# GpSimd issues the loads of the first three sample states ahead of its subtractions for the input projection

## The chip, the cores and the metric

The kernel runs on one core of a Trainium2 chip. The metric is the device time of one execution in microseconds; the time of a kernel is the median of its runs. The engines of the core are TensorE (PE; its weight loads are PEld), VectorE (DVE), ScalarE (ACT), GpSimd (POOL) and SyncE (SP). SP and GpSimd issue the transfers: SP's go through the DMA queue q1, GpSimd's through q0, and both queues are served by the same 16 DMA engines.

## What is computed

One inference step of a two-layer decoder for a prompt of 256 tokens and 8 sample tokens, 264 tokens in all, in float32. The part that matters here is the first layer's mLSTM mixer:

```python
proj = x @ w_in + b_in
x_m, o_pre, i_pre, f_pre = jnp.split(proj, [A_INNER, 2 * A_INNER, 2 * A_INNER + A_HEADS], axis=-1)
x_c = silu(causal_conv(x_m))                      # 4 taps along the tokens
q, k = x_c @ w_q[h], x_c @ w_k[h] * A_HEAD_DIM ** -0.5
v = x_m @ w_v[h]
log_i, log_f = i_pre, log_sigmoid(f_pre)
h, C, n, m = mlstm_chunkwise(q, k, v, log_i, log_f, C0, n0, m0)   # C <- decay * C + (ws * k)^T v
h = sigmoid(o_pre) * h
return h @ w_out, new_conv, C, n, m
```

A_INNER is 2048, there are 4 heads of 512. Each of the 8 sample tokens brings its own matrix memory C0 for each head: 32 states of 512x512 float32, 1 MB each, which are read, decayed, updated and written back. The second layer is sliding-window attention, and both layers end in a large mixture of experts (PEER), which takes most of the span.

## The kernel before

All weights that are streamed lie in HBM as units of 128 x 1024 float32 (512 KB). SP loads them in order into a ring of four buffers (`raw`): the first four at once, each further one when the unit four places earlier has been used (L380). Between the first four and the loop, SP issues x (after the first unit), then the inputs of the gate products (w_gate, b_gate, m_in, sel4, sel8: L362, five transfers on one semaphore, gate_in), then const, cols, cols_a, conv_in and some small ones.

Units 0 to 31 are the input projection. For each of them ScalarE rounds the weights to a high part (L862), GpSimd subtracts to get the low part (the function `lows`, L1608; two subtractions of 128x512 a unit), and TensorE does three products a chunk (high by high, high by low, low by high). After units 0 and 1 TensorE does the 32 products for the gates (L558), which wait for gate_in. ScalarE then computes the gate values (L996 to L1001), VectorE scans them (from L1388), and then does the convolution over the x_m channels (L1411, L1413), chunk by chunk as the projection delivers them.

Units 32 to 37 belong to head 0 and are used as plain float32 by TensorE: 32 to 35 hold W_q and W_k, 36 and 37 the two halves of W_v (`project_v`). Unit 36 is issued by SP when unit 32 has been used, 37 when 33 has, and so on. After them TensorE goes on with the prompt's scores and the steps over the sample states (`sample_step`), which ScalarE decays first (L1064).

GpSimd's program is one sequence. Before the change: the 64 subtractions of `lows(U_IN, U_QKV)`, the loads of states 0 to 2 (L1613) into the buffer `cs` (part of `big`), the store of the new m (L1615), the store of the convolution's tail (L1617), the store of the rows of the attention's relative bias to HBM, each row repeated 128 times (`bias_rows`, L1620, 3 MB), which waits until VectorE has written them (bias_rows_kept, L1423), the loads of states 3 and 4 into `halves` (L1624), which wait for the last use of the split weights, and then the loop over the 32 states (L1629, L1638). Nothing else uses `cs` before the loads.

Of the kernel before, what the change touches and what calls it, by code (L numbers as in the profile page):

```python
# [59 lines left out]
U_IN = 0  # L60
U_QKV = U_IN + 2 * IC
# [26 lines left out]
def n_split(n):  # L88
    return _before(n, "pool", "dve")
# [41 lines left out]
def _build(nc, io, ctx):  # L131
# [5 lines left out]
    def sem(name):  # L137
        if name not in sems:
            sems[name] = ctx.enter_context(nc.semaphore(name))
        return sems[name]  # L140
# [5 lines left out]
    sizes = [("big", n_big), ("raw", RING * 1024), ("halves", 4096), ("xh", n_x), ("xl", n_x), ("scb", 4096),  # L146
             ("top", 528 + 2 * 256 + 2 * 128 + 384 + 768), ("const", NCONST), ("cols", NCOLS)]
    total = sum(n for _, n in sizes)
    sb("arena", [P, total])
    base = nc.sbuf_base - 4 * total  # L150
# [1448 lines left out]
    def _(pool):  # L1599
        def lows(a, b):  # L1600

            n0 = n_split(a)
            with pool.Fori(0, (b - a) // RING) as it:
                for k in range(RING):
                    for half in range(2):
                        v, o = 2 * ((n0 + k) % 2) + half, slice(half * 512, (half + 1) * 512)
                        pool.wait_ge(high_done, it * (2 * RING) + (2 * (n0 + k) + half + 1))
                        nc.gpsimd.tensor_tensor(split[:, v, 1, :], ring[:, (a + k) % RING, o], split_f[:, v, 0, :],  # L1608
                                                ALU.subtract).then_inc(low_done["pool"], 1)

        lows(U_IN, U_QKV)
        for n in range(3):
            pool.dma_start(cs[:, n], io["state_in"][n]).then_inc(sem(f"state_in_{n}"), 16)  # L1613
        pool.wait_ge(sem("m_kept"), 1)
        pool.dma_start(io["m_out"], m_out[0:HA, :]).then_inc(sem("small_out"), 16)  # L1615
        pool.wait_ge(sem("conv_kept"), 1)
# [216 lines left out]
```

## Time and profile before

| | us |
|---|---|
| median of 3 runs | 2440.13 |
| lowest run | 2440.05 |
| the profiled execution, its own time | 2439.59 |
| its span, from the first to the last instruction | 2437.8 |
| TensorE busy | 2311.4 (95%) |
| VectorE busy | 1576.5 (65%) |
| ScalarE busy | 1136.2 (47%) |
| GpSimd busy | 918.6 (38%) |

In the profile, times are microseconds from the start of the span, those of single instructions ns where marked. The granted clock of TensorE is given as a share of full speed: 1.00 is 2.4 GHz and 0.50 is 1.2 GHz. Engine names with a q (SPq, POOLq) are an engine's queue of instructions, where DMA issues are counted.

### The profile page before, as it was taken

The page shows a single profiled execution, that of the slowest core. Times are in us where ns is not written, and L with a number is a line of the kernel's source. Part 1 is how long each engine was busy: PE and PEld are TensorE (multiplying, and loading weights), DVE is VectorE, ACT ScalarE, POOL GpSimd, SP SyncE. Part 2 cuts the span into 40 slices and gives each one's busy share as a digit, 9 for nine tenths or more (in the row PEclk, how much of TensorE's full clock was granted, in tenths as well). Part 3 has the DMA queues.
Part 4 walks back from the last instruction along what each step waited for, and adds up shares of the span by engine and source line. Part 5 has one row for each costly group of instructions (what it writes and reads, how often), then busy time and mean ns, then how long its engine had stood idle before and what let it go on. Part 6 is the DMA issues. An engine that isn't in the chain of part 4 may idle for free.

```text
span 2437.8 us, 51606 instructions
## 1 busy us (share of the span) xinstructions
PE 2311.4 (95%) x17330; PEld 2141.1 (88%) x17330; DVE 1576.5 (65%) x3494; ACT 1136.2 (47%) x2231; POOL 918.6 (38%) x754
## 2 busy tenths in 40 slices
PE   7889999989999999999999888899989999999997
PEld 6854555789999999999999877899989999999997
DVE  6404544319996999755555644189969997555555
ACT  5523333156654444455555542556544444555554
POOL 5621111077976666200000150779866662000000
PEclk9999999999999999999999988999989999999999
DMA  4487777544544444455555631545434444555552
GB/s 159 138 235 306 296 296 293 194 161 147 181 164 138 138 138 138 143 180 179 179 180 181 198 126 66 164 147 182 167 130 138 138 138 143 180 179 180 180 180 103
DMA packets 105491, 420.81 MB, mean 173 GB/s; under 512 B 12101, under 2 KB 12701, under 8 KB 95945
## 3 DMA queue, kind: packets, MB, share of 16 engines
q1 hardware_dynamic: 92728, 335.28, 40.9%
q0 software_dynamic: 12400, 83.47, 9.8%
q8 instruction: 45, 0.74, 0.1%
q10 hardware_dynamic: 288, 1.08, 0.1%
q14 instruction: 30, 0.25, 0.0%
HBM read 375.14 MB, written 44.63 MB: 172 GB/s over the span
## 4 chain that ended last, share of the span: by engine, by line
PE 76%; DVE 17%; issue 3%; POOL 2%; ACT 1%; DMA 1%; POOLq 0%; ACTq 0%; DVEq 0%; SPq 0%
PE pa L390 48%; PE pb L390 27%; DVE top L1220 4%; DVE top L1217 3%; POOL split L1608 2%; DVE pa L1260 1%; DVE pa L1259 1%; DVE top L1262 1%; DVE scb L1223 1%; DMA raw<-in_units 1%; DVE pb L1223 1%; DVE scb L1237 0%; DVE big L1437 0%; DVE top L1239 0%; DVE top L1256 0%
## 5 line engine op out<-in xcount | busy, mean ns | idle before, releaser
L862 ACT CAST split<-raw 128x512 fp32r<-128x512 f32 x1176 | 721.0, 619 | 928.0 <-PE pa L390 650.0
L390 PE MATMUL pa<-xh,split 128*128 128x264 f32 x5280 | 997.4, 288 | 64.1 <-DVE xl L1202 23.9
L1608 POOL TENSOR_TENSOR split<-raw,split 128x512 fp32r<-128x512 f32 x664 | 869.8, 1320 | 328.6 <-ACT split L862 306.8
L390 PEld LDWEIGHTS pa<-xh,split 128*128 128x128 f32 x5280 | 836.1, 191 | 69.6 <-POOL split L1608 30.1
L390 PE MATMUL pa<-xl,split 128*128 128x264 f32 x2640 | 755.5, 286 | 0.0
L1209 DVE TENSOR_TENSOR split<-raw,split 128x512 fp32r<-128x512 f32 x512 | 354.3, 693 | 302.3 <-ACT split L862 302.3
L390 PEld LDWEIGHTS pa<-xl,split 128*128 128x128 f32 x2640 | 506.0, 192 | 0.0
L390 PE MATMUL pa<-wsplit,split 128*128 128x264 f32 x3072 | 416.6, 285 | 6.6 <-DVE wsplit L1355 6.6
L390 PE MATMUL pb<-wsplit,split 128*128 128x264 f32 x3072 | 415.0, 284 | 0.0
L390 PEld LDWEIGHTS pa<-wsplit,split 128*128 128x128 f32 x3072 | 391.9, 189 | 6.9 <-issue 6.9
L390 PEld LDWEIGHTS pb<-wsplit,split 128*128 128x128 f32 x3072 | 390.9, 188 | 0.0
L1303 DVE TENSOR_SCALAR scb<-pa,top 128x128 f32<-128x128 f32 x528 | 173.6, 397 | 0.0
L1318 DVE TENSOR_TENSOR big<-big,top 128x264 f32 (+1 forms) x128 | 144.0, 1125 | 39.7 <-ACT top L921 26.1
L390 PE MATMUL pa<-big,raw 128*128 128x264 f32 x640 | 150.4, 390 | 2.5 <-ACT big L1048 1.7
L390 PEld LDWEIGHTS pa<-big,raw 128*128 128x128 f32 x640 | 119.6, 190 | 37.0 <-issue 16.6
L1657 POOL DMA_DIRECT2D big<-in_kw_in x1 | 1.2, 1195 | 388.3 <-DVE big L1182 388.3
L390 PE MATMUL pb<-scb 128*128 128x128 f32 (+2 forms) x1080 | 133.9, 276 | 0.0
L390 PEld LDWEIGHTS pb<-scb 128*128 128x128 f32 (+1 forms) x1080 | 127.2, 191 | 1.2 <-issue 0.9
L1355 DVE TENSOR_TENSOR wsplit<-big,wsplit 128x264 fp32r<-128x264 f32 x256 | 109.3, 427 | 1.1 <-ACT wsplit L970 1.1
L970 ACT CAST wsplit<-big 128x264 fp32r (+1 forms) x256 | 104.6, 409 | 6.0 <-DVE big L1311 6.0
L390 PE MATMUL pb<-big 128*128 128x128 f32 (+6 forms) x514 | 101.3, 369 | 3.8 <-ACT big L911 3.2
L390 PEld LDWEIGHTS pb<-big 128*128 128x128 f32 (+3 forms) x514 | 67.1, 181 | 39.8 <-issue 31.4
(238 smaller groups left out, 1655.9 us busy)
## 6 DMA issues: line engine op xcount, KB each, us to landing
raw<-in_units SPq DMA_DIRECT2D x636, 512.0 KB, 3.3
big<-in_state_in POOLq DMA_DIRECT2D x20, 1024.0 KB, 8.1
out_state_out<-big POOLq DMA_DIRECT2D x20, 1024.0 KB, 5.3
halves<-in_state_in POOLq DMA_DIRECT2D x12, 1024.0 KB, 9.0
out_state_out<-halves POOLq DMA_DIRECT2D x12, 1024.0 KB, 5.2
out_c_prompt<-big POOLq DMA_DIRECT2D x4, 1024.0 KB, 5.1
bias_rows<-scb POOLq DMA_DIRECT2D x1, 3072.0 KB, 39.3
big<-in_skeys POOLq DMA_DIRECT2D x2, 1024.0 KB, 6.8
```

The source lines that it names most:

```text
L390: return pe.matmul(out, lhs, rhs, start=start, stop=stop)
L862: nc.scalar.copy(split[:, 2 * (n % 2) + half, 0, :], ring[:, slot, half * 512:(half + 1) * 512]).then_inc(high_done, 1)
L970: nc.scalar.copy(wsplit[:, i % 4, 0, :], big[:, bass.ds(it * (4 * T) + i * T, T)] if it is not None else w3[:, i, :]).then_inc(sem("w_high ...
L1209: V.tensor_tensor(split[:, 2 * (n % 2) + half, 1, :], ring[:, slot, o], split_f[:, 2 * (n % 2) + half, 0, :], ALU.subtract).then_inc(low_d ...
L1217: last = V.max(s[:, o], v)
L1220: last = V.max_index(i[:, o], s[:, o], v)
L1223: last = V.match_replace(v, s[:, o], v, LOWEST)
L1259: link(V.tensor_tensor(eq, rank.to_broadcast([n, nk, TOPK]), i16, ALU.is_equal))
L1303: last = V.tensor_scalar(hot[:, s % 2, 0, t, :], iota_p, i_col, g_col, ALU.is_equal, ALU.mult)
L1318: V.tensor_tensor(w, w, gelu[:, i % RING, :], ALU.mult).then_inc(sem("row_gated"), 1)
L1355: V.tensor_tensor(wsplit[:, i % 4, 1, :], big[:, bass.ds(it * (4 * T) + i * T, T)], wsplit_f[:, i % 4, 0, :], ALU.subtract).then_inc(sem(" ...
L1608: nc.gpsimd.tensor_tensor(split[:, v, 1, :], ring[:, (a + k) % RING, o], split_f[:, v, 0, :], ALU.subtract).then_inc(low_done["pool"], 1)
```

## The change

The loop that issues the loads of states 0 to 2 moves from behind the 64 subtractions to the head of GpSimd's program. Its three DMAs, their targets and their semaphores stay the same, and no wait is added or taken away.

```diff
-        lows(U_IN, U_QKV)
         for n in range(3):
             pool.dma_start(cs[:, n], io["state_in"][n]).then_inc(sem(f"state_in_{n}"), 16)
+        lows(U_IN, U_QKV)
         pool.wait_ge(sem("m_kept"), 1)
         pool.dma_start(io["m_out"], m_out[0:HA, :]).then_inc(sem("small_out"), 16)
```

On GpSimd, at the head of its program (the memsets of constants at L1801 come first, the branch and the ISA instruction at L1603 open the loop of `lows`):

```order
 L1801 MEMSET const-uint8-127 128x1
 L1598 UNCONDITIONAL_BRANCH
+L1612 DMA big<-in_state_in 128x2048 x3
 L1603 UNCONDITIONAL_BRANCH
 L1603 ISA
```

The three loads stand ahead of the loop with the subtractions, right behind the constants. At the other end of that loop, where the input projection hands over to the heads:

```order
 L1603 REGISTER_ALU
 L1603 COMPARE_AND_BRANCH
-L1613 DMA big<-in_state_in 128x2048 x3
 L1615 DMA out_m_out<-big 4x9
 L1617 DMA out_conv_out<-big 128x432
```

The stores of m and of the convolution's tail, and after them that of the bias rows, now follow the last subtraction directly. The order on the other four engines is the same.

## Rows read from the trace of the kernel before

**Rows 1.** The page, busy time of each engine (share of the span) and instructions.
```profile
PE 2311.4 (95%) x17330; PEld 2141.1 (88%) x17330; DVE 1576.5 (65%) x3494; ACT 1136.2 (47%) x2231; POOL 918.6 (38%) x754
```

**Rows 2.** The chain of work that ended last, 130 to 520 us: start, length, what.
```profile
145.79 21.04 DMA raw<-in_units
```

**Rows 3.** Timeline of PE, 154 to 178: start, length, instruction, [idle before <-releaser].
```profile
154.20 5.72 PE L390 MATMUL pb<-raw,big 128*128 128x512 f32 x12
166.88 8.55 PE L390 MATMUL pb<-raw,big 128*128 128x512 f32 x12 [6.96 <-DMA raw<-in_units]
```

**Rows 4.** Busy time by stretch; the last columns are granted clock, DMA share, GB/s.
```profile
165.00:170.00 5.00, 3.12 (x4) 1.18 (x4) 0.00 (x0) 0.00 (x0) 0.00 (x0) 0.50 0.99 171
```

**Rows 5.** Timeline of GpSimd, 130 to 140.
```profile
133.28 1.75 POOL L1613 DMA_DIRECT2D big<-in_state_in  x3
135.02 0.52 POOL L1615 DMA_DIRECT2D out_m_out<-big  x1
...
136.79 1.05 POOL L1620 DMA_DIRECT2D bias_rows<-scb  x1 [0.70 <-DVE scb L1423]
137.83 1.06 POOL L1624 DMA_DIRECT2D halves<-in_state_in  x2
```

**Rows 6.** Issues of L1613 with times to landing; DMA issues, 133 to 152, bias_rows (landing last).
```profile
L1613 POOL DMA_DIRECT2D big<-in_state_in x3: 527/546/699, 133.3 to 134.5; - x3
...
DMA to landing us min/median/max: 6.3/8.1/10.7
...
bias_rows<-scb POOLq DMA_DIRECT2D x1, 3072.0 KB, 39.3
```

**Rows 7.** DMA issues at 141.4, 145.8 and 150.2 (units 36, 37, 38): us to landing last.
```profile
raw<-in_units SPq DMA_DIRECT2D x1, 512.0 KB, 10.5
...
raw<-in_units SPq DMA_DIRECT2D x1, 512.0 KB, 21.0
...
raw<-in_units SPq DMA_DIRECT2D x1, 512.0 KB, 23.8
```

**Rows 8.** DMA queues, 152 to 158, then 158 to 166: packets, MB, share of engines.
```profile
q0 software_dynamic: 130, 0.60, 96.4%
q1 hardware_dynamic: 4, 0.02, 0.7%
...
q0 software_dynamic: 164, 0.76, 80.2%
q1 hardware_dynamic: 157, 0.58, 17.8%
```

**Rows 9.** Busy time by stretch, columns as in rows 4 (GB/s last).
```profile
2.00:12.00 10.00, 4.15 (x19) 4.18 (x20) 4.37 (x12) 4.83 (x13) 4.54 (x4) 1.00 1.01 378
136.00:145.00 9.00, 8.43 (x45) 7.00 (x44) 0.65 (x4) 1.06 (x3) 2.20 (x4) 1.00 1.00 385
```

**Rows 10.** SP's issues of const and cols_a at the start, and their times to landing.
```profile
5.15 0.36 SPq L363 DMA_DIRECT2D const<-in_const  x1
...
const<-in_const SPq DMA_DIRECT2D x1, 192.0 KB, 6.9
...
6.04 0.45 SPq L365 DMA_DIRECT2D big<-in_cols_a  x1
...
big<-in_cols_a SPq DMA_DIRECT2D x1, 124.0 KB, 6.4
```

**Rows 11.** Timeline of all engines, 0 to 30.
```profile
4.64 2.48 POOL L1608 TENSOR_TENSOR split<-raw,split 128x512 fp32r<-128x512 f32 x2 [4.18 <-ACT split L862]
...
6.75 2.60 ACT L903 CAST xh<-big 128x264 fp32r<-128x264 f32 x8 [1.67 <-DMA big<-in_x]
...
14.07 0.46 ACT L1022 ACTIVATE big<-pa,big 128x256 f32<-128x256 f32 x1
...
15.78 7.28 PE L390 MATMUL pb<-big 128*4 128x264 f32 x32
```

**Rows 12.** Timeline of VectorE, 26 to 35.
```profile
26.75 0.42 DVE L1388 SCALAR_TENSOR_TENSOR scb<-scb 4x264 f32<-4x264 f32 x1 [13.36 <-ACT scb L1001]
```

**Rows 13.** Busy time in the convolution's stretch: PE, PEld, DVE, ACT, POOL.
```profile
34.60:91.50 56.90, 39.90 (x292) 38.60 (x290) 53.47 (x68) 34.13 (x87) 33.39 (x24) 0.93 0.36 120
```

**Rows 14.** Timeline of ScalarE, 118 to 200: the first decay of a state.
```profile
154.96 2.00 ACT L1064 ACTIVATE big<-big 128x2048 f32<-128x2048 f32 x1
```

## The prediction

> **What bounds the kernel now.** I read the page first: TensorE is busy 95% of the span, so microseconds are lost only where it stands still or runs at its half clock [rows 1]. The change touches two stretches, the first 25 us and the hand-over from the input projection to the heads of the mLSTM (133 to 182 us), so I read these from the chain of waits, the timelines and the packets of the two DMA queues.
>
> In the second stretch the chain holds one wait for a transfer: a weight unit issued at 145.79 that lands 21.04 us later [rows 2]. Units 0 to 31 are the input projection, 32 to 35 hold W_q and W_k of head 0, 36 and 37 its W_v. TensorE runs unit 36 from 154.20 in 5.72 us, stands still for 6.96 us for unit 37, and then needs 8.55 us for the same twelve instructions [rows 3], because the granted clock is at its lower level, 0.50 (1.2 GHz), after the stand [rows 4]. The place costs 6.96 + (8.55 - 5.72) = 9.8 us. That is the most that any edit here can win.
>
> Why unit 37 is late: GpSimd issues 3 state loads from 133.28, the broadcast of bias rows at 136.79, and two more state loads [rows 5]. The three states take until 134.5 + 10.7 = 145.2, and bias_rows until 136.8 + 39.3 = 176.1, so it has the engines for 30.9 us behind the states [rows 6]. Unit 36, issued at 141.4, lands after 10.5 us; unit 37 after 21.0; unit 38, issued at 150.2, after 23.8, which is 7.2 us behind unit 37 [rows 7]. From 152 to 158 the queue of the units (q1) moves 4 packets and GpSimd's (q0) 130, though unit 37 had been issued at 145.8; from 158 to 166 they move 157 and 164 [rows 8]. So a unit issued into a backlog of bias_rows waits some 12 us for its first packet and then shares the engines packet by packet.
>
> **The change, part by part.**
>
> *The loads at the start.* Three DMAs of 1024 KB are 3.15 MB. The engines are full from 2 to 12 us at 378 GB/s, and the same loads ran at 385 GB/s at 136 to 145 [rows 9]; both show 16 engines at their limit, so all that stands behind the loads in a queue is put off by 3.15 MB / 0.385 MB per us = 8.2 us. If part of the SP queue gets past, it is less; I take 7.9 and keep 7.5 to 8.3. Who is hit? The inputs of the gate products stand in the SP queue just ahead of const, which is issued at 5.15 and lands after 6.9, so at 12.05 at the latest [rows 10]. TensorE starts the 32 gate products at 15.78 and needs 7.28 us [rows 11]: 3.7 us are spare. 12.05 + 7.9 = 19.95, so the gate products begin 4.2 us later (3.8 to 4.6).
>
> What else is late lies under that wait. x lands near 6.7, when ScalarE starts on it [rows 11]; if it shares its last half with a state, it comes some 2 us later, and units 0 and 1 end at 15.8 + 2 = 18, still ahead of 19.95. cols_a, issued at 6.04 with 6.4 us to landing, goes from 12.4 to 20.3 [rows 10]; ScalarE's first evacuation at 14.07 [rows 11] then comes at 20.3, and what it has left ahead of the gates is two pairs of casts and evacuations, a few us, done before the gate products end at 27.2. GpSimd's issue work, 133.28 to 135.02 for three, 1.75 us [rows 5], falls into the 4.18 us for which it waits before its first subtraction at 4.64 [rows 11].
>
> Is the 4.2 us given back later? VectorE waits 13.36 us for the gate values and only then goes on to the scans and the convolution [rows 12]; from 34.6 to 91.5 it is busy 53.47 of 56.9 us while TensorE is busy 39.9 [rows 13]. The stage is VectorE's, it starts from the gates, and it has no slack. The cost is carried in full. Whether TensorE loses its clock over 1.7 to 4 us of standing there, no row settles; nothing is the lower bound and 2.83 us (the price in rows 3) the upper one, and I take nothing.
>
> *The place the loads leave.* GpSimd gets to its stores 1.75 us sooner, but bias_rows waits for VectorE (0.70 us before it in rows 5) and is still issued at 136.79. Its packets no longer stand behind three states. The first state was issued at 133.28 and the engines are full from 136, so 2.7 us after an issue is a fair start: bias_rows runs from 139.5 rather than 145.2, and ends 5.7 us earlier, near 170.4. The states' own landing was waited for by nobody: the first decay, at 154.96, has no wait before it [rows 14].
>
> What does that do to units 36 and 37? Unit 36 is issued at 141.4, now 2 us into bias_rows, as unit 37 was before (145.8 against 145.2). Before, it slipped in with the first packets of bias_rows. So its time to landing lies between its own 10.5 us and unit 37's 21.0, and its place in the backlog is that of unit 37; I take 19.6, so 161.0 (160 to 162.4), where TensorE wants it at 154.20. Unit 37 follows in the same queue by the 7.2 us of its successor: 168.2. TensorE: stands 154.2 to 161.0, runs unit 36 at the lower clock in 8.55 to 169.6, then unit 37 in 5.72 to 175.3. Before, it was done at 166.88 + 8.55 = 175.43. The stall moves from the second half of W_v to the first, and the gain is 0.1 us (with unit 36 at 160 and 162.4: 1.1 and -1.3). What comes behind (units 38 to 40, states 3 and 4) lands earlier and nobody waits for it.
>
> **The sum.** The profiled execution took 2439.59, of which the span is 2437.8. 2439.6 + 4.2 - 0.1 = 2443.7. The median lies 0.5 above that execution; I forecast 2444.0. By the bounds of these terms alone (start 3.8 to 4.6, clock 0 to 2.83, gain -1.3 to 1.1) the likeliest case spans 2442 to 2448; its own range is 2441.5 to 2447.
>
> **Rivals.**
>
> *Fair sharing from the first packet.* If the units alternate with bias_rows as soon as they are issued, unit 36 lands well before 154.2 and unit 37 before 159.9, the stall goes, and the whole 9.8 us are won: 2439.6 + 4.2 - 9.8 = 2434.0. For it: from 158 to 166 the queues do alternate [rows 8]. Against it: the 4 packets against 130 just before. It decides where unit 36's time to landing falls under 12.8 us (154.2 - 141.4). Chance 0.20. The Trainium skill (DMA: Bandwidth & Descriptors, section Queues, rings and completion order) states this rule: each DMA engine goes round the queues it has work for, a packet at a time. By that rule the time would be the one just given; the trace agrees with it from 158 on and not in the six us before.
>
> *In between.* Unit 36 lands some 14 to 17 us after its issue, at 155 to 158. The stand shrinks to 1 to 4 us plus what unit 37 adds, and 3 to 7 us are won: 2437 to 2441. Chance 0.13.
>
> *The start costs nothing.* If GpSimd's packets come only behind what SP has issued, the gate inputs land at 12 as now, and the time stays near 2440. For it: GpSimd's first packets came 2.7 us after an issue, and SP has four transfers out by then. Against it: the alternation in rows 8, and the gate inputs stand behind three units in their queue, so all three states fit in ahead of them. Chance 0.08; together with fair sharing, near 2430, 0.02.
>
> *The slower side: TensorE goes cold at the gates.* If its granted clock falls over the longer stand, the 7.28 us of gate products cost 2.83 us more (rows 3) up to their whole length again: 2446.5 to 2451. It decides from a stand that is long enough; the one of 6.96 us was [rows 3, 4], here it is 2 to 4 us. Chance 0.07.
>
> **How the numbers follow.** The likeliest case keeps 0.50; with the five rivals that makes 1. I give 2433.5 to 2447.0: it holds the likeliest case, fair sharing, the case in between and the free start, some 0.9 before the errors of the terms. No term reaches 2% (49 us), which is about what a measurement of this kernel can tell from no change, so within 2% has 0.98, and 0.01 stands on either side for what I have not seen.
>
> **What would show it.** In the changed profile: the gate products start near 20 instead of 15.78 and const lands some 8 us later (the start, right or wrong); VectorE's first scan near 31 instead of 26.75 (carried); the wait for a weight unit stands before the first half of W_v, near 158 on the shifted clock, with 12 instructions at the lower level behind it, and bias_rows lands after about 33 us instead of 39.3 (the moved stall). A unit 36 that lands in under 12 us proves fair sharing and makes the forecast wrong by its whole gain; gate products at 15.8 make it wrong at the start.

## The result, and the profile after

The changed kernel takes 2448.61 us (median of 7 runs, 2444.9 to 2449.78) against 2441.28 for the kernel before: a ratio of 1.0029, with a 95% interval of 1.0017 to 1.0041. It is 7.3 us slower; that is far within the 2% of the prediction's classes, but 1.6 us above the upper end of its range and 4.6 above its number. The profiled execution of after took 2446.84 us, with a span of 2445.0, so the pair of profiles stands 7.25 us apart, about as far as the medians. One of the seven executions of before took 2849.49 us and is left out of the ratio; without it the median of before is 2440.83.

The page of after gives the same picture as [rows 1], with 2.9 us more of busy TensorE:

```profile
PE 2314.3 (95%) x17330; PEld 2142.8 (88%) x17330; DVE 1576.8 (64%) x3494; ACT 1139.0 (47%) x2231; POOL 918.6 (38%) x754
```

**The start.** This is the timeline of after, from 0 to 34 us: start, length, engine and line, operation, and in brackets the idle time before it with what ended it. It answers to [rows 10 to 12].

```profile
1.29 1.76 POOL L1612 DMA_DIRECT2D big<-in_state_in  x3 [0.83 <-POOLq L1801]
...
4.91 2.48 POOL L1608 TENSOR_TENSOR split<-raw,split 128x512 fp32r<-128x512 f32 x2 [1.87 <-ACT split L862]
...
5.11 0.36 SPq L363 DMA_DIRECT2D const<-in_const  x1
...
6.98 3.33 SPq L367 DMA_DIRECT2D big<-in_n_in  x1
10.36 3.20 SPq L368 DMA_DIRECT2D big<-in_rel_bias  x1
...
7.82 2.61 ACT L903 CAST xh<-big 128x264 fp32r<-128x264 f32 x8 [2.47 <-DMA big<-in_x]
...
19.40 7.28 PE L390 MATMUL pb<-big 128*4 128x264 f32 x32 [2.09 <-DMA scb<-in_sel]
...
20.98 0.47 ACT L1022 ACTIVATE big<-pa,big 128x256 f32<-128x256 f32 x1
...
30.38 0.42 DVE L1388 SCALAR_TENSOR_TENSOR scb<-scb 4x264 f32<-4x264 f32 x1 [9.51 <-ACT scb L1001]
```

The loads go out at 1.29 and GpSimd's first subtraction is only 0.27 us later, so issuing them is covered. What is not covered are the gate inputs: TensorE stands 2.09 us for the last of them (in_sel) and starts the gate products at 19.40 instead of 15.78. VectorE's first scan follows, at 30.38 instead of 26.75. x lands 1.07 us later (the first cast is at 7.82 instead of 6.75). The issue list of const and the packets of the two queues from 7 to 17 us (packets, MB, share of the engines) show the reason:

```profile
const<-in_const SPq DMA_DIRECT2D x1, 192.0 KB, 14.4
...
q0 software_dynamic: 381, 2.78, 65.9%
q1 hardware_dynamic: 397, 1.44, 35.2%
```

const needs 14.4 us to its landing instead of 6.9. The two queues move nearly as many packets, but GpSimd's are larger (2.78 MB in 381 of them against 1.44 MB in 397), so the state loads get two thirds of the bytes and SP's queue one third.

**The hand-over.** The timeline of GpSimd in after, 130 to 200 us, answers to [rows 5]:

```profile
136.22 0.56 POOL L1615 DMA_DIRECT2D out_m_out<-big  x1
136.78 0.57 POOL L1617 DMA_DIRECT2D out_conv_out<-big  x1
139.73 1.05 POOL L1620 DMA_DIRECT2D bias_rows<-scb  x1 [2.38 <-DVE scb L1423]
140.76 1.07 POOL L1624 DMA_DIRECT2D halves<-in_state_in  x2
```

bias_rows is issued 2.94 us later than before, which is how late the projection ends. Next come the DMA issues of after at 139.7, 144.35 and 148.73 (bias_rows, units 36 and 37; us to landing last), and the packets of 144.4 to 156 and of 160 to 166. They answer to [rows 6 to 8].

```profile
bias_rows<-scb POOLq DMA_DIRECT2D x1, 3072.0 KB, 35.1
...
raw<-in_units SPq DMA_DIRECT2D x1, 512.0 KB, 21.7
...
raw<-in_units SPq DMA_DIRECT2D x1, 512.0 KB, 23.8
...
q0 software_dynamic: 250, 1.15, 96.0%
...
q0 software_dynamic: 127, 0.59, 81.4%
q1 hardware_dynamic: 126, 0.45, 18.4%
```

Unit 36 now takes 21.7 us where it took 10.5. From 144.4 to 156 there is one queue only: 250 packets of bias_rows and none of the units, with unit 36 issued at 144.35. From 160 on the queues alternate, 127 against 126.

In before the same unit met the state loads. Between its issue at 141.42 and its first packet, 263 of GpSimd's packets with 1.33 MB, most of it state loads, went in 3.9 us; then it alternated with bias_rows and was through by 151. In after 295 packets with 1.36 MB went ahead of it, all of bias_rows, and they took 13.4 us. These are the queues (packets, MB, share) of before, 141.4 to 145.3 and 145.4 to 150.9, and of after, 144.35 to 157.8:

```profile
q0 software_dynamic: 263, 1.33, 99.0%
...
q0 software_dynamic: 146, 0.67, 81.3%
q1 hardware_dynamic: 138, 0.52, 23.1%
...
q0 software_dynamic: 295, 1.36, 97.7%
```

In before the packets of unit 36 moved while unit 37, issued at 145.79, got none until 157.6. So it is the newly issued unit that waits, not the whole queue.

TensorE's timeline, 138 to 200 us, shows where it stands (compare [rows 3]):

```profile
153.50 3.80 PE L390 MATMUL pa<-big,raw 128*128 128x264 f32 x16 [0.57 <-ACT big L1048]
166.22 13.94 PE L390 MATMUL pb<-raw,big 128*128 128x512 f32 x24 [8.92 <-DMA raw<-in_units]
```

The stand has moved from between the halves of W_v to ahead of both, and grown from 6.96 to 8.92 us. W_v ran from 154.20 to 175.43 before, 21.23 us with its stand; now it is 157.30 (153.50 + 3.80) to 180.16, 22.86 us. By stretch (the last columns are granted clock, DMA share, GB/s) the clock is low behind the stand, as in [rows 4], and then full:

```profile
166.50:171.50 5.00, 5.00 (x7) 1.02 (x6) 0.00 (x0) 0.00 (x0) 0.00 (x0) 0.54 1.01 178
172.00:178.00 6.00, 6.00 (x14) 1.76 (x13) 0.00 (x0) 0.00 (x0) 0.00 (x0) 1.00 0.99 369
```

So the 7.25 us between the two profiles are: 3.1 at the start of W_v (157.30 against 154.20), 1.6 in W_v (22.86 against 21.23), and 2.5 that come later, where the two programs are the same.

### The profile page after: what moved, and what is told of

Its sections match the earlier page's. It is cut to its first block, busy times and chain, and to the rows that moved or that the text cites. A ratio compares the mean times of both kernels' runs of the same rounds, so it can differ in the third digit from the quotient of the medians.

```text
span 2445.0 us, 51606 instructions
## 1 busy us (share of the span) xinstructions
PE 2314.3 (95%) x17330; PEld 2142.8 (88%) x17330; DVE 1576.8 (64%) x3494; ACT 1139.0 (47%) x2231; POOL 918.6 (38%) x754
## 4 chain that ended last, share of the span: by engine, by line
PE 75%; DVE 17%; issue 4%; POOL 2%; ACT 1%; DMA 1%; POOLq 0%; ACTq 0%; DVEq 0%; SPq 0%
PE pa L390 48%; PE pb L390 27%; DVE top L1220 4%; DVE top L1217 3%; POOL split L1608 2%; DVE pa L1260 1%; DVE pa L1259 1%; DVE top L1262 1%; DVE scb L1223 1%; DMA raw<-in_units 1%; DVE pb L1223 1%; DVE scb L1237 0%; ACT big L890 0%; DVE big L1437 0%; DVE top L1256 0%
## 5 line engine op out<-in xcount | busy, mean ns | idle before, releaser
L1318 DVE TENSOR_TENSOR big<-big,top 128x264 f32 (+1 forms) x128 | 144.1, 1126 | 39.6 <-ACT top L921 26.0
```

The lines of the kernel that those rows point to most:

```text
L1318: V.tensor_tensor(w, w, gelu[:, i % RING, :], ALU.mult).then_inc(sem("row_gated"), 1)
```

## The experiments

The theory going in was the prediction's: the start delays the gates, and at the hand-over a unit issued into the packets of bias_rows waits some 12 us for its first packet, whichever unit it is. The rivals were that the state loads and not bias_rows hold the units up, that the late x rather than the gate inputs makes the start late, and that a delay at the start is partly won back. All times are medians; the kernel before took 2441.51 us beside e1 to e4, 2440.44 beside e6 to e9 and 2440.65 beside e10 to e12. Intervals are 95% of the ratio. Each kernel has one profiled execution, and a time read from a profile carries its scatter: the eight kernels in which nothing is put ahead of the gate products' inputs (before, e1, e2, e6, e8, e10, e11 and e12) begin them anywhere between 15.29 and 16.65 us.

### Where the loads stand: e1_mid, e3_one_first, e11_after_four

The three loads behind the subtractions of the first eight units:

```diff
-        lows(U_IN, U_QKV)
+        lows(U_IN, U_IN + 8)
         for n in range(3):
             pool.dma_start(cs[:, n], io["state_in"][n]).then_inc(sem(f"state_in_{n}"), 16)
+        lows(U_IN + 8, U_QKV)
```

> The three loads stand after the subtractions for the first eight units instead of at the head (about 47 us into the span); all else as in the changed kernel. Theory A (the start costs about 3.6 us because the loads hold up the gate inputs; the hand-over costs about 1.8 us more than before because bias_rows starts sooner and catches unit 36): the gate products start at 15.8 as before, no cost at the start; TensorE stands for 8 to 9 us ahead of the first half of W_v; 2441 to 2445 us. Theory B (fair sharing once the states are out of the way of bias_rows; the whole loss comes from the start): no stand ahead of W_v, 2430 to 2433 us. Theory C (the cost at the start is not the gate inputs but GpSimd's issuing): as A.

Measured: 2444.7 us, 1.0016 (1.0007 to 1.0025), 3.2 us slower. The gate products start at 15.67, so the start costs nothing, as expected. But it is not free on the way: the loads go out from 46.72, and VectorE's next three instructions of the convolution take 6.19 us instead of 4.37. These are rows of VectorE's timeline in e1_mid, the three together and the first alone:

```profile
48.48 6.19 DVE L1413 SCALAR_TENSOR_TENSOR big<-big 128x288 f32<-128x288 f32 x3
...
48.48 4.17 DVE L1413 SCALAR_TENSOR_TENSOR big<-big 128x288 f32<-128x288 f32 x1
```

and of before, the same three, and (busy time, mean ns) the two of that shape from 53 on:

```profile
48.53 4.37 DVE L1413 SCALAR_TENSOR_TENSOR big<-big 128x288 f32<-128x288 f32 x3
...
L1413 DVE SCALAR_TENSOR_TENSOR big<-big 128x288 f32<-128x288 f32 x2 | 1.0, 520 | 0.1
```

bias_rows is issued 2.45 us later than before (139.24 instead of 136.79), by which time the projection is done. At 48.58 GpSimd, which had been issuing, runs four subtractions in a row. In before it runs five in a row there (7.23 us from 45.35), so the row of subtractions alone is not the difference. In before an instruction of VectorE takes some 1.43 us beside these subtractions and 0.52 where none runs. So a subtraction beside it slows VectorE; why one instruction takes 4.17 us right behind the issue of the loads was not tested. At the hand-over TensorE stands 8.49 us ahead of W_v, and W_v is done 3.2 us late:

```profile
165.31 13.34 PE L390 MATMUL pb<-raw,big 128*128 128x512 f32 x24 [8.49 <-DMA raw<-in_units]
```

One load at the head, two at the old place:

```diff
+        for n in range(1):
+            pool.dma_start(cs[:, n], io["state_in"][n]).then_inc(sem(f"state_in_{n}"), 16)
         lows(U_IN, U_QKV)
-        for n in range(3):
+        for n in range(1, 3):
             pool.dma_start(cs[:, n], io["state_in"][n]).then_inc(sem(f"state_in_{n}"), 16)
```

> One of the three loads stands at the head, two stay at the old place. Theory A (a third of the bytes puts the gate inputs off by a third of the 7.5 us, 2.5 us, which is less than their 3.7 us to spare): gate products start within 0.5 us of 15.8; bias_rows starts 2.5 us sooner than before, so unit 36 is issued about when it begins, as unit 36 was before, and the stand stays near 7 to 9 us: 2439 to 2444 us. Rival C (any load at the head costs its share): gate products 1.2 us later, 2442 to 2445 us.

Measured: 2445.23 us, 1.0015 (1.0006 to 1.0024), above the range that was expected. The gate products start at 17.30, 1.5 us later than in before and 0.65 later than the latest of the kernels with nothing ahead, where the expectation had them within 0.5 us. The gate inputs do not hold them (there is no wait ahead of them). x comes late: its cast is at 7.80, 1.05 us late with a single state beside it, and units 0 and 1 end later. In after the same delay lies under the wait for the gate inputs, whose 2.09 us are the rest of its 3.62. At the hand-over the stand is 8.56 us, unit 36 takes 21.4 us, and W_v is done 2.4 us late. Its first packets come 4.1 us after its issue, behind the two states, but by 156.4 there are only 8 of them; the rest follow from 156.5 on.

```profile
17.30 7.28 PE L390 MATMUL pb<-big 128*4 128x264 f32 x32
...
164.74 13.10 PE L390 MATMUL pb<-raw,big 128*128 128x512 f32 x24 [8.56 <-DMA raw<-in_units]
```

The loads behind the subtractions of the first four units, which brings them out at 19.6 us, between the start and the convolution:

```diff
-        lows(U_IN, U_QKV)
+        lows(U_IN, U_IN + 4)
         for n in range(3):
             pool.dma_start(cs[:, n], io["state_in"][n]).then_inc(sem(f"state_in_{n}"), 16)
+        lows(U_IN + 4, U_QKV)
```

> The three loads stand behind the subtractions for the first four units (near 19 us, when the gate inputs have landed, and ahead of a stretch with nearly no transfers); all else as in the changed kernel. Theory A: x, gate products and convolution at the times of the kernel before, no cost at the start; the stand still comes ahead of the first half of W_v and costs 1 to 2 us more than before: 2441 to 2444 us. Rival (GpSimd's issuing or the bytes cost the same anywhere): 2446 us or more.

Measured: 2443.52 us, 1.0009 (1.0000 to 1.0018), 2.9 us slower (0.0 to 4.4). x comes as before (6.86), the gate products start at 16.35, within the scatter, and the projection ends 0.8 us late; the stand ahead of W_v is 8.98 us and W_v is done 3.2 us late:

```profile
164.16 14.50 PE L390 MATMUL pb<-raw,big 128*128 128x512 f32 x24 [8.98 <-DMA raw<-in_units]
```

What follows from the three: unit 36 takes 21.3, 21.4 and 21.8 us, and 21.7 in after, as soon as even one state load has left the hand-over. Its delay does not depend on where the loads go. The stand ahead of W_v is 8.49 to 8.98 us in all four, against 6.96 before. Stand and products together take 21.8, 21.7, 23.5 and, in after, 22.9 us, against 21.2 before: 0.4 to 2.3 more, the products' part (13.10 to 14.50 us) varying with the clock behind the stand. In e6 and e10 below, where the loads stay in place, unit 36 takes 10.6 and 10.2 us, and stand and products together 21.5 and 20.9. So that unit 36 is late without the loads is shown; what TensorE loses by it is small, and its size is uncertain: with the start left nearly alone (e11) the displaced loads cost 2.9 us by the medians, of which the projection's end has 0.8, and the interval reaches down to nothing.

### A delay at the gates alone: e10_shift8, e6_shift16

Both are the kernel before with extra products of the same shape ahead of the gate products, into a part of the bank that nobody reads.

```diff
         pe.wait_ge(sem("gate_in"), 80)
+        for i in range(8):
+            mm(pb[0:HA, 2, 0:T], w_gate[:, i % DC, 0:HA], x[:, i % DC, :], i == 0, i == 7)
```

> The kernel before, with 8 more products of the gates' shape ahead of the gate products. (In e6_shift16 the sixteen products were as many as all the gate products, 7.28 us, twice what was stated for it: a record counts half a product.) Here they are 3.64 us, the same delay of the gates as in the changed kernel, with no transfer moved. Theory D (a delay of the gates is carried to the end one to one, within what TensorE's clock adds or takes): 2443 to 2446 us. Rival F (a delay is partly taken back): under 2443 us.

Measured: 2444.37 us, 1.0015 (1.0006 to 1.0024). In before 32 products took 7.28 us; here 48 instructions (the 8 calls are 16 of them) take 10.85, so the delay is 3.6 us, and the time is 3.7 us longer (1.5 to 5.9).

```profile
15.36 10.85 PE L390 MATMUL pb<-big 128*4 128x264 f32 x48
```

The double (its expectation counts the 16 calls as 3.64 us; they are 32 instructions and take 7.1):

```diff
         pe.wait_ge(sem("gate_in"), 80)
+        for i in range(16):
+            mm(pb[0:HA, 2, 0:T], w_gate[:, i % DC, 0:HA], x[:, i % DC, :], i == 0, i == 15)
```

> The kernel before, with 16 more products of the gates' shape on TensorE ahead of the gate products (into a bank that nothing reads), which is half of their 7.28 us: everything behind starts 3.6 us later and no transfer is moved. Theory D (a pure delay at the start is carried one to one): 2445 us, 3.6 over the kernel before. Rival E (a delay also moves the later stretches at TensorE's lower clock, so that more or less than the delay arrives at the end): anything else, 2443 to 2450 us, with the shift against the kernel before growing or shrinking behind 200 us.

Measured: 2448.09 us, 1.0032 (1.0020 to 1.0044), 7.65 us longer (4.9 to 10.7) for a delay of 14.41 - 7.28 = 7.1:

```profile
15.31 14.41 PE L390 MATMUL pb<-big 128*4 128x264 f32 x64
```

By the medians a delay of the gates comes out at the end one to one, at 3.6 us and at twice that, within intervals of 2 to 3 us each way. In the profile of e10 the gate products end 3.15 us late, the projection 2.84 and the span 2.5. In that of e6 they end 6.66 us late and the projection 6.25; behind it the shift moves between 5.5 and 7.6, as Rival E said that it might, and it is 7.55 at the end. So most of the delay is carried, a few tenths are won back in the projection, and what comes later belongs to TensorE's clock (see below).

### The gate inputs ahead of units 2 and 3: e7_after_gate_first

The kernel after, with the five transfers of gate_in issued behind unit 1 instead of behind unit 3:

```diff
-        for k in range(1, RING):
-            sp.dma_start(ring[:, k, :], io["units"][k]).then_inc(landed[k], 16)
+        sp.dma_start(ring[:, 1, :], io["units"][1]).then_inc(landed[1], 16)
         for dst, name in ((w_gate, "w_gate"), (b_rows[0:HA, :], "b_gate"), (m_in[0:HA, :], "m_in"),
...
             sp.dma_start(dst, io[name]).then_inc(sem("gate_in"), 16)
+        for k in range(2, RING):
+            sp.dma_start(ring[:, k, :], io["units"][k]).then_inc(landed[k], 16)
```

> The changed kernel, in which SP issues the five gate inputs behind unit 1 instead of behind unit 3. Theory A (the gate products wait for gate_in): that wait of 2.09 us goes, gate products start near 17.3 instead of 19.4 us, where x, which still shares with the states, and unit 1 set them; 2445 to 2448 us, 1 to 2.5 us under the changed kernel. Rival C (the delay is that of x and unit 1): gate products stay at 19 us or later, no gain.

Measured: 2444.85 us, 1.0019 (1.0010 to 1.0029), 4.4 us above before where after stands 7.3 above it. The gate products start at 17.42 with no wait ahead of them, the 2 us of stand are gone, and what is left of the delay is that of x, as in e3. This shows that the gate inputs' place in SP's queue makes 2 of the 3.6 us at the gates. The two times alone would not show it: their intervals, 2.4 to 7.1 and 4.2 to 10.0 us above before, overlap.

```profile
17.42 7.29 PE L391 MATMUL pb<-big 128*4 128x264 f32 x32
```

### bias_rows later, in one piece: e2_bias_late, e4_after_bias_late

The kernel before, with the store of bias_rows behind the loads of states 3 and 4 and held until W_v's units have been used:

```diff
+        pool.wait_ge(halves_used, 2 * (U_QKV - U_IN))
+        for n in range(3, SLOTS):
+            pool.dma_start(state(n), io["state_in"][n]).then_inc(sem(f"state_in_{n}"), 16)
         pool.wait_ge(sem("bias_rows_kept"), 1)
+        pool.wait_ge(units_used, 6)
...
-        pool.wait_ge(halves_used, 2 * (U_QKV - U_IN))
-        for n in range(3, SLOTS):
-            pool.dma_start(state(n), io["state_in"][n]).then_inc(sem(f"state_in_{n}"), 16)
```

> The kernel before, in which the store of bias_rows stands behind the loads of states 3 and 4 and waits until units 32 to 37 have been used. Theory A (bias_rows alone is what makes a W_v unit late): units 36 and 37 land within 10 us of their issue although five states stand in front of them, TensorE does not stand ahead of W_v, the 9.8 us of the stand and of the lower clock are won, unless state 0 going out behind bias_rows stalls the sample steps: 2430 to 2434 us. Rival B (the states in front make unit 37 late): the stand stays, 2438 to 2443 us.

Measured: 2442.51 us, 1.0004 (0.9995 to 1.0013). The time is outside the range of Theory A (2430 to 2434), though the units behave as it said. With all five states ahead of it and no bias_rows, unit 36 lands in 7.9 us and TensorE runs W_v without a stand in 11.47 us, done 8.4 us earlier than before:

```profile
155.55 11.47 PE L390 MATMUL pb<-raw,big 128*128 128x512 f32 x24
```

But bias_rows, issued at 167.70, now stands in the way of the traffic of the first state steps. GpSimd's timeline of e2, 160 to 235 us, shows it waiting 22.35 us until the first new state has been stored, before it may load the next one into that buffer, and 9.24 us at a later one:

```profile
167.70 1.05 POOL L1624 DMA_DIRECT2D bias_rows<-scb  x1 [29.14 <-PE pb L390]
177.62 0.54 POOL L1630 DMA_DIRECT2D out_state_out<-big  x1 [8.88 <-DVE big L1437]
182.94 0.54 POOL L1630 DMA_DIRECT2D out_state_out<-big  x1 [4.78 <-DVE big L1437]
205.83 0.53 POOL L1639 DMA_DIRECT2D big<-in_state_in  x1 [22.35 <-DMA out_state_out<-big]
...
218.82 0.53 POOL L1639 DMA_DIRECT2D big<-in_state_in  x1 [9.24 <-DMA out_state_out<-big]
```

By 227 us the whole gain has been given back (VectorE's step that starts at 226.34 in before starts at 226.71 in e2). The same edit on the kernel after, that is e2 with

```diff
-        lows(U_IN, U_QKV)
         for n in range(3):
             pool.dma_start(cs[:, n], io["state_in"][n]).then_inc(sem(f"state_in_{n}"), 16)
+        lows(U_IN, U_QKV)
```

> The changed kernel, with the store of bias_rows moved as in e2_bias_late. It leaves only what the change does at the start. Theory A: no stand ahead of W_v, and e2_bias_late's time plus 2.9 to 3.6 us, 2433 to 2438 us. Rival B (the start costs nothing that lasts, the loss is in the hand-over): e2_bias_late's time.

Measured: 2448.35 us, 1.0026 (1.0015 to 1.0036), 5.8 us above e2, where 2.9 to 3.6 were expected. Here too W_v runs without a stand and is done 6.6 us early, and the state steps take it back. In the profiles e4 is 1.8 us behind e2 at the end of W_v and 4.2 behind it after the steps that wait for bias_rows, so this pair does not give the start's price by itself.

### bias_rows later, in sixteen pieces: e8_bias_pieces, e9_after_bias_pieces, e12_after_four_pieces

The kernel before, with bias_rows cut into 16 stores of 8 copies each, one behind each of the state steps 8 to 23:

```diff
-        pool.dma_start(io["bias_rows"], rt[0:HB, :].rearrange("p (o w) -> p o w", o=1).to_broadcast(
-            [HB, P, BIASW])).then_inc(sem("bias_stored"), 16)
...
+                if 8 <= n < 24:
+                    pool.dma_start(io["bias_rows"][:, 8 * (n - 8):8 * (n - 7), :],
+                                   rt[0:HB, :].rearrange("p (o w) -> p o w", o=1).to_broadcast(
+                                       [HB, 8, BIASW])).then_inc(sem("bias_stored"), 16)
...
+        pool.wait_ge(sem("bias_stored"), 256)
         pool.wait_ge(sem("ln_sum"), DC)
         load_skeys(0)
...
-        pool.wait_ge(sem("bias_stored"), 16)
+        pool.wait_ge(sem("bias_stored"), 256)
```

The first of the two waits is new: GpSimd's next loads after the state steps (skeys) now stand behind the last piece.

> The kernel before, in which the store of bias_rows is cut into 16 stores of 8 of its 128 copies, one behind each of the steps 8 to 23 over the states. Theory A (bias_rows costs the stand of 9.8 us where it is, and gives back what it wins where it is put in one piece): units 36 and 37 in time, each piece holds a state up by about 2 us, which the sample steps hide for the most part: 2430 to 2436 us. Rival (the steps over the states have no room for 31 us of transfers): 2437 us or more.

Measured: 2431.88 us, 0.9963 (0.9951 to 0.9976), 8.6 us faster than before. Unit 36 takes 8.0 us and unit 37 6.9, W_v runs from 153.40 without a stand, and this time most of the gain lasts to the end (W_v was done 10.6 us early, of which 0.8 came from ahead of the hand-over). The issues of units 36 and 37 in e8:

```profile
raw<-in_units SPq DMA_DIRECT2D x1, 512.0 KB, 8.0
...
raw<-in_units SPq DMA_DIRECT2D x1, 512.0 KB, 6.9
```

The state loads stand ahead of unit 36 here just as in before. So of the two suspects it is bias_rows that makes the units late for TensorE. e8 differs from e2 in two ways, the size of the pieces and their later place; which of them keeps the gain was not separated.

The same with the change of this case:

```diff
-        lows(U_IN, U_QKV)
         for n in range(3):
             pool.dma_start(cs[:, n], io["state_in"][n]).then_inc(sem(f"state_in_{n}"), 16)
+        lows(U_IN, U_QKV)
```

> The changed kernel with the store of bias_rows cut up as in e8_bias_pieces. Theory A: e8_bias_pieces plus the cost at the start of 2.9 to 3.6 us: 2433 to 2440 us. Rival B (with bias_rows away, having the first three states early wins something): e8_bias_pieces or less.

Measured: 2435.89 us, 0.9979 (0.9970 to 0.9988), 4.0 us above e8. With the hand-over out of the account, this is the best figure here for the price of the three loads at the start; e4 against e2 gave 5.8 with the state steps in it. In the profiled execution of e9 one thing was seen that after does not have: the gate products took 8.97 us instead of 7.28.

```profile
19.51 8.97 PE L390 MATMUL pb<-big 128*4 128x264 f32 x32 [2.43 <-DMA scb<-in_sel]
```

Its row by stretch, 18 to 22 us, shows a granted clock of 0.74, where that of after shows 1.00:

```profile
18.00:22.00 4.00, 2.49 (x7) 0.86 (x8) 0.36 (x1) 1.99 (x5) 1.29 (x1) 0.74 1.07 358
```

And e8 with the loads behind the first four units, as in e11:

```diff
-        lows(U_IN, U_QKV)
+        lows(U_IN, U_IN + 4)
         for n in range(3):
             pool.dma_start(cs[:, n], io["state_in"][n]).then_inc(sem(f"state_in_{n}"), 16)
+        lows(U_IN + 4, U_QKV)
```

> As e11_after_four, with the store of bias_rows cut up as in e8_bias_pieces. Theory A: nothing left for the early loads to win or to lose, the time of e8_bias_pieces within 2 us: 2429 to 2434 us. Rival G (the states being early wins a part of the hand-over): under 2429 us.

Measured: 2431.38 us, 0.9962 (0.9949 to 0.9976): 9.3 us faster than before, where e8 was 8.6 faster, which is no difference. With bias_rows out of the way, early states neither win nor lose (the two medians lie 0.5 us apart): the loads at their old place cost nothing that shows here. e11, with bias_rows where it was, is 2.9 us slower than before (0.0 to 4.4). In the profiles unit 36 lands after more than 21 us only where both hold, at least one of the loads gone and bias_rows there.

## Why the prediction was too low

The direction and the places were right: no change by the 2%, a few us slower, from the gates and from a stand that moves ahead of W_v. Two steps failed: unit 36 was given 19.6 us to its landing and takes 21.7, and everything behind W_v was put at nothing, where the profiles differ by 2.5 us.

**The start: right in size.** const was put 7.5 to 8.3 us later and came 7.5 later; the gate products near 20, and they start at 19.40; ScalarE's first evacuation (its copy of a finished product, L1022) at 20.3, and it comes at 20.98; the scan near 31, and it is at 30.38. The term of 4.2 us measured 3.6 at the gates and 4.0 by the medians (e9 against e8). That it is carried in full holds for a pure delay by the medians (e10, e6); in the pair of profiles, the projection ends 2.9 to 3.1 us late, so some 0.5 us of the 3.6 were given back there. The step that puts x under the wait for the gates holds in after, but only there: in e3 and e7, where that wait is gone, the gate products are still 1.5 and 1.6 us late with x.

**The hand-over: the term that failed.** The prediction took 19.6 us for unit 36, with 10.5 and 21.0 as its ends, and got a gain of 0.1. It takes 21.7 in after and 21.3 to 21.8 in e1, e3 and e11, all above the upper end. The reasoning was that its place in the backlog is that of unit 37 before. The runs show that it is no better than that, and a little worse. Unit 36 waited for 1.33 MB of GpSimd's in before and for 1.36 MB in after; it was not the amount that changed but what it was, mostly state loads, which took 3.9 us, in before, and bias_rows alone, which took 13.4 us, in after. With two of the three loads left (e3) it already takes 21.4 us. On the clock of after (3.1 us late) W_v was to end at 175.3 + 3.1 = 178.4 and ends at 180.16. This step is worth 1.7 of the 3.1 us between the profile's forecast of 2443.7 and the 2446.84 that it took; the cheaper start takes 1.1 off, and the stretches behind W_v add 2.5.

**What is left: a term that the sum did not have.** The 2.5 us after the end of W_v lie in stretches where both programs are the same, and they come in steps that go both ways. The largest is at 740 us, where TensorE returns from a stand. It stands for 10.92 us in both profiles and returns at 736.38 in before and at 741.98 in after, 5.60 us late. VectorE's L1292, which waits for these products, is then 7.03 us late. Here are this instruction and the row by stretch of the 12 us around TensorE's return, of before:

```profile
744.71 0.98 DVE L1292 COPY top<-pb 128x792 f32<-128x792 f32 x1 [7.72 <-PE pb L494]
...
736.00:748.00 12.00, 11.62 (x85) 11.44 (x86) 4.25 (x8) 5.45 (x12) 9.21 (x8) 0.87 0.48 156
```

and of after:

```profile
751.74 0.98 DVE L1292 COPY top<-pb 128x792 f32<-128x792 f32 x1 [9.16 <-PE pb L494]
...
741.60:753.60 12.00, 11.62 (x73) 11.44 (x74) 2.81 (x4) 4.79 (x11) 8.29 (x7) 0.73 0.38 131
```

The same stand is followed by more time at the lower level in one profile than in the other: a mean granted clock of 0.87 and of 0.73. This is no price of the loads as transfers: e6, which moves none, is late by the same step (5.97 us before it, 7.40 behind it), and e10 is not (2.5 on both sides). The kernel before itself scatters by as much: its 23 runs beside e6 to e9 lie between 2438.21 and 2443.35 us, the six quickest at a mean clock of 0.970 or 0.971 and the five slowest at 0.967 or 0.968. By the medians, the start (4.0) and the displaced loads (e11, 2.9, which has 0.8 of start in it) give 6.1 of the 7.3 us. The remaining 1.2 is inside what these intervals, about 2.3 us wide each way, leave open. Whether some executions of after run the gate products at the lower clock, as the one of e9 did, would be a further part; only one execution of each kernel is profiled, and this stays open.

**The rivals.** Fair sharing from the first packet is refuted (none of the 250 packets from 144.4 to 156 is the unit's), and with it the case in between. That is the rule that the Trainium skill states (DMA: Bandwidth & Descriptors, section Queues, rings and completion order): a DMA engine goes round its queues a packet at a time. The trace of after agrees from 160 on, 127 packets against 126, and does not in the first 11.6 us after the unit's issue, if the trace's packets are those of the rule and the engines had the unit's work by then; no run shows either. A free start is refuted by the 3.62 us at the gates. TensorE cold at the gates did not happen in the profile of after (7.28 us) or in that of e4 (its gate products also take 7.28); it did in that of e9, for 1.7 us. There it cost less than the 2.83 us that the rival took as its lower price.

**The range.** The bounds of the terms reached to 2448.3 for the profiled execution, 2448.8 with the 0.5 that the forecast adds for the median, and the range was cut at 2447 without a reason. The wider bounds would have held the 2448.61 by luck, through 2.83 us for a cold clock at the gates that the profile of after does not have. The sum also missed a hand-over 0.3 us worse than its worst bound (1.6 lost where -1.3 was the end) and the later 2.5 us: the median and the lowest run of before that were known lay 0.08 us apart, and its scatter of 5 us was seen only in later runs.

## What to carry to other kernels

Before a transfer is moved to an earlier place, ask what it kept apart where it stood: here the state loads, which nobody waited for, were what let a weight unit through ahead of a broadcast. At the head of this program the DMA engines are full [rows 9], and what is put in front delays the first inputs: one state made the gate products 1.5 us late (e3), three made them 3.6 us late, and most of such a delay arrives at the end (e10, e6). It pays to look at where the small inputs of a long chain stand: moving them ahead of two units took 2 of these 3.6 us away (e7). And when a bulk store holds up other transfers, moving it whole only moved the stand (e2), while pieces of it, issued between later steps, removed it (e8, 0.9963).

## What the hardware showed that was not expected

- **A newly issued unit waited for about the same amount of GpSimd's transfers, slow or fast.** From the issue of unit 36 to its first packet, GpSimd's queue moved 1.33 MB in before, 1.40 MB in e8 (without bias_rows) and 1.36 MB in after (bias_rows alone), in 3.9, 3.5 and 13.4 us. For unit 37 in before, issued while unit 36 was alternating with bias_rows, it was 1.27 MB in 11.8 us. That a fixed amount goes first, and takes long where the transfer is slow, is a reading that fits; it was not tested, and in e3 the unit's packets begin after 1.00 MB and only 8 of them come before a second gap. The queue of e8, 140.6 to 144.1:

```profile
q0 software_dynamic: 260, 1.40, 102.6%
```

- **bias_rows is slow in itself.** Its 250 packets in 11.6 us are 1.15 MB with the engines 96% busy, 99 GB/s, where the engines moved 385 GB/s at about the same share while the state loads ran [rows 9].
- **SP's own issue can stall.** With three states ahead in the engines, the issues of n_in and rel_bias took 3.33 and 3.20 us on SP instead of 0.44 each, and the first reload of the ring came at 14.71 us instead of 8.78.
- **A stand of 2.1 to 2.4 us came with a lower clock once and without it once.** The gate products began at a mean granted clock of 0.74 behind a stand of 2.43 us in e9, and at 1.00 behind 2.09 us in after.
